# Weight loads in quarters in front of nearly every projection unit, and a running count of equal scores in two halves

## What is computed

```
h = _rmsnorm(x, norm_g[l])
p = h @ w_in[l]
oa = _chunk_band_attention(...) * silu(az)      # A: softmax attention over a band
ob = _hgrn2(...) * silu(bz)                     # B: gated linear recurrence
oc = _dsa(...) * silu(cz)                       # C: indexer, top 256 keys, attention
od = _rwkv7(...) * silu(dz)                     # D: delta-rule state
y = sum over the branches of sigmoid(gate) * (o @ w_branch[l, branch])
x = x + y @ w_out[l]
```

## Time and profile before

| | us |
|---|---|
| median of 3 runs | 2764.34 |
| lowest and highest | 2760.86, 2766.89 |
| time of the profiled execution | 2762.82 |
| its span, first to last instruction | 2761.0 |
| PE busy in the span | 2716.2 |

### The profile page before, as it was taken

How to read it: one execution, slowest core, us unless ns; L and a number is a source line. 1 busy time by engine, 2 the same in 40 slices (tenths; PEclk the granted TensorE clock), 3 DMA queues, 4 the chain that set the end, 5 groups by cost and what they waited for, 6 DMA issues and landing times.

```text
span 2761.0 us, 46225 instructions
## 1 busy us (share of the span) xinstructions
PE 2716.2 (98%) x18624; PEld 1465.9 (53%) x18624; DVE 1595.5 (58%) x3018; ACT 973.2 (35%) x1869; POOL 802.5 (29%) x582
## 2 busy tenths in 40 slices
PE   8999999999999999999999999999999999999999
PEld 4447444466574565544444464544665745755443
DVE  4689876754508732265337898767545178232753
ACT  3455665321224224500124556643112332344001
POOL 3333312411334332133033333124113443321420
PEclk9999999999999999999999999999999999999999
DMA  4221111211111223183142121112111112232731
GB/s 163 68 59 50 46 35 53 70 45 45 47 42 39 63 82 102 32 281 116 41 123 57 46 62 39 36 49 71 50 37 47 46 43 66 70 107 79 246 111 46
DMA packets 135612, 200.90 MB, mean 73 GB/s; under 512 B 8392, under 2 KB 90472, under 8 KB 134632
## 3 DMA queue, kind: packets, MB, share of 16 engines
q1 hardware_dynamic: 116808, 163.86, 19.8%
q10 hardware_dynamic: 18592, 34.09, 3.3%
HBM read 146.53 MB, written 44.59 MB: 69 GB/s over the span
## 4 chain that ended last, share of the span: by engine, by line
PE 44%; DVE 4%; ACT 1%; issue 1%; POOL 0%; DVEq 0%; ACTq 0%
PE ps L498 23%; PE ps L495 4%; PE ps L757 4%; PE ps L771 3%; PE ps L1163 1%; PE ps L1152 1%; PE ps L1498 1%; PE ps L1176 1%; DVE arena L1898 1%; DVE arena L1640 1%; PE ps L2018 1%; PE ps L2112 1%; PE ps L2010 0%; DVE arena L1624 0%; PE ps L1964 0%
## 5 line engine op out<-in xcount | busy, mean ns | idle before, releaser
L498 PE MATMUL ps<-hT,wr 128*128 128x512 f32 x1856 | 858.9, 600 | 3.1 <-PEq L2574 2.8
L498 PEld LDWEIGHTS ps<-hT,wr 128*128 128x128 f32 x1856 | 338.7, 191 | 375.6 <-issue 367.1
L498 PE MATMUL ps<-sums,wr 128*128 128x512 f32 x928 | 438.4, 600 | 1.1 <-ACT gts L568 0.7
L673 POOL TENSOR_TENSOR gts<-gts,wr 128x512 f32<-128x512 f32 x96 | 153.7, 1601 | 621.0 <-ACT wr L549 400.7
L1252 DVE CUSTOM_DVE_ANT_0 arena<-ps,arena 128x640 f32<-128x640 f32 (+7 forms) x128 | 90.5, 707 | 334.1 <-PE ps L1152 317.4
L498 PEld LDWEIGHTS ps<-sums,wr 128*128 128x128 f32 x928 | 167.2, 190 | 180.9 <-issue 171.6
L549 ACT ACTIVATE wr<-ps 128x512 f32<-128x512 f32 x174 | 103.2, 593 | 369.7 <-PE ps L498 324.2
L757 PE MATMUL ps<-xo,arena 128*128 128x512 f32 x512 | 220.1, 592 | 0.0
L498 PE MATMUL ps<-wr 128*128 128x512 f32 x464 | 218.5, 600 | 0.0
L1640 DVE TENSOR_SCALAR_CACHE_REDUCE arena<-arena,sm 128x384 f32<-128x384 uint16 (+7 forms) x256 | 192.8, 809 | 2.2
L642 POOL TENSOR_TENSOR wr<-wr 128x512 f32<-128x512 f32 x57 | 81.2, 1425 | 382.9 <-PE ps L498 347.7
(11 more groups left out here) (321 smaller groups left out, 4139.2 us busy)
## 6 DMA issues: line engine op xcount, KB each, us to landing
wr<-in_w_in SPq DMA_DIRECT2D x36, 1024.0 KB, 5.5
gate_tanh<-gts ACTq DMA_DIRECT2D x128, 256.0 KB, 3.3
arena<-gate_tanh SPq DMA_DIRECT2D x128, 256.0 KB, 2.9
wr<-in_w_in SPq DMA_DIRECT2D x104, 256.0 KB, 2.8
wr<-in_w_in SPq DMA_DIRECT2D x16, 512.0 KB, 3.8
arena<-in_w_branch SPq DMA_DIRECT2D x8, 1024.0 KB, 7.7
wr<-in_w_out SPq DMA_DIRECT2D x8, 1024.0 KB, 7.4
arena<-arena SPq DMA_DIRECT2D x36, 128.0 KB, 2.6
```

The source lines that it names most:

```text
L498: ins = pe.matmul(ap, lhsT=right(u, w_side)[:, kt, :], rhs=left(h_side, kt), start=fresh and kt == 0, stop=kt == half_k - 1, skip_group_ch ...
L673: pool.tensor_tensor(dst, dst, stage_of(u), ALU.add).then_inc(sg("pool_added"), 1)
```

## The change

```diff
             def load_parts(n):
 
                 u = next(u for u in range(len(units)) if n in units[u][1])
-                return 4 if units[u][0] == "gate" and units[u - 1][0] == "gate" else 1
+                return 4 if u >= 2 and n == units[u][1][0] and len(units[u - 1][1]) == 1 else 1
...
-                        key = done if q == 0 else (*fill_done[n - 1][0][:3], q - 1)
+                        key = done if q == 0 else (*fill_done[n - 1][0][:3], 2 * q - 2)
...
-                    ap = jobs.open(pe, key, T)
+                    ap = jobs.open(pe, key, S2[0] if g and u + 1 == len(units) else T)
...
-                    v256 = cbits[:, j:j + 1]
+                    v256, middle = cbits[:, j:j + 1], P * (i + 1) // 2
...
                     elif step == 1:
                         link(dve, dve.tensor_scalar(equal, sc, v256, None, ALU.is_equal))
+                        link(dve, dve.tensor_tensor_scan(sc[:, 0:middle], equal[:, 0:middle], equal[:, 0:middle], 0.0, ALU.add, ALU.max))
                     elif step == 2:
-                        link(dve, dve.tensor_tensor_scan(sc, equal, equal, 0.0, ALU.add, ALU.max))
+                        link(dve, dve.tensor_tensor_scan(sc[:, middle:], equal[:, middle:], equal[:, middle:], sc[:, middle - 1:middle], ALU.add, ALU.max))
```

## The result

| | before | changed |
|---|---|---|
| median, lowest and highest, us | 2765.61 (2760.86 to 2766.99) | 2786.06 (2781.81 to 2788.53) |
| profiled execution, its span | 2762.82, 2761.0 | 2788.53, 2786.7 |
| PE busy | 2716.2 | 2724.8 |
| PE idle in the span | 44.8 | 61.9 |

The changed kernel takes 1.0075 times as long, 95% interval 1.0058 to 1.0093: 20.5 us more between the medians. The direction and the first link of the mechanism are those forecast, the size is twice that forecast: 2775 was said, and 2786.06 lies just under the upper end of the range (2787). The profiled execution is the slowest of the four, 25.7 us over that of before; of these PE's idle time is 17.1 and its busy time 8.6.

A forecast was written before the change was run, and what follows sets the result against it. PE was taken as the bound, busy 2716.2 of 2761.0 us. From 2762.82, +14.8 for stalls at unit ends (7.4 a layer), -0.9 for the scan and -1.5 for the L2010 gap gave 2775.2, forecast 2775, range 2764 to 2787.

The forecast's parts named there:

- The chain: Unit ends: late last quarter delays POOL's t1, its addition, ACT's copy, then PE's bank; 6.1 us against 6.70, 7.1 beside a store.
- two gates with POOL free: Layer 0 gates, product 4 ending at 491.7 and 893.64: load lands in 3.8 beside a store, PE stalls 0.35 us each.
- gate in D: Product 4 ended at 543.35: DVE's 128x2048 addition holds POOL up, so the copy is late and PE stalls 1.55 us.
- B0: Unit end, product 4 ended at 745.23: 3.4 us stall if POOL and DVE take turns, 1.2 if POOL sums in one go.
- gate in B: DVE's row of sums, which held up POOL's addition, would hit t1 too and delay the addition 1.27; stall 0.75 us.
- A's attention: Product 4 ended at 1079.56, store beside the load: ACT's work comes 1.4 late, PE stalls 0.9 to 1.0 us.
- rival 3: ACT's delay spreads: search starts 1.8 us later and PE pays, plus three delays of 0.5; +5 a layer, 2785; chance 0.13.
- C's index: First turns queue behind POOL's later additions, 1.8 us later in sum; DVE idles there several times, so taken as 0.
- C's search: ACT's copies come 0.4 to 0.7 late in three units; even 2 us covered by DVE's 8.81 us idle before the attention.
- The attention of C: One late-ACT end like the one in A's attention, with less in it: stall 0.0 to 0.2 us.
- The gap at L2010: PE's 3.0 us gap beside a 1 MB load, perhaps delayed program fetches; half taken as returning, -1.5 us.
- The scan: Scan halved in C's attention, 2.28 us becoming about 1.2 and 1.2: removes one PE wait; -0.9 us, bounds -1.0 and +0.3.

## Why the prediction was right, and where it was too small

**The chain was right.** The waits of a layer that the prediction named, and what came of them (the wait of PE in layer 0 of the changed kernel, against the term):

| end | term | measured |
|---|---|---|
| two gates with POOL free | 0.35 each | 0.13, 0.43 |
| gate in D | 1.55 | 0.28 + 0.89 |
| B0 | 3.4 | 3.35 |
| gate in B | 0.75 | none |
| A's attention | 1.0 | 1.08 |

Together the waits for L549 and the added ones for L1233 are 11.8 us in both layers, where the sum had 14.8. In B0 the choice between 3.4 and 1.2 was right: the two engines took turns. The lock rule of the Trainium skill (SBUF — State Buffer, section Who interferes with whom) holds in that the loser waits for the whole instruction: POOL's sums of 1.26 took 3.27 and 3.31 beside DVE operations of 2.29 and 3.24.

**The gate in B** failed by its step "the same will hit t1". In the earlier trace rows the addition was shut out by a run of short DVE operations for 3.89 us. In the changed kernel it was the other way round:

```profile
945.91 1.42 POOL L642 TENSOR_TENSOR wr<-wr 128x512 f32<-128x512 f32 x1 [18.25 <-DMA wr<-in_w_in]
946.12 1.75 DVE L1859 TENSOR_TENSOR arena<-arena 128x512 f32<-128x512 f32 x1
947.29 1.71 POOL L673 TENSOR_TENSOR gts<-gts,wr 128x512 f32<-128x512 f32 x1
```

t1 got in at once and DVE's operation waited for it. Which of them gets the port when is not to be read from one instance. (The term had a slip too: it gives the copy 0.70 to spare and then takes off 0.54; with 0.70 it is 0.57, no longer 0.75.)

**The sum was too small, because of what was taken as 0.** Three estimates failed, and rival 3 (ACT's delay spreads into the search and the index, 2785) was the place. That its time is so near the 2786 measured is luck: its own terms, 1.8 and three of 0.5, make 3.3 a layer and 2782, where it says 5 a layer, and the search and the index cost 6.3 in both layers:

- C's index: "DVE idles there several times, and I take 0". POOL's later sums run beside DVE's operations of the index, ACT waits for these, and its copy and PE's next scores come late, 0.44 and 0.68 in a layer, 2.3 in both. In the timeline of the changed kernel, where the same operation of 384 had taken 0.62 before:

```profile
100.97 1.37 POOL L652 TENSOR_TENSOR wr<-wr 128x512 f32<-128x512 f32 x1
101.26 1.50 DVE L1614 SCALAR_TENSOR_TENSOR arena<-arena,sm 128x384 f32<-128x384 f32 x1
102.79 0.60 ACT L549 ACTIVATE wr<-ps 128x512 f32<-128x512 f32 x1 [1.86 <-DVE arena L1614]
102.96 1.13 PE L1499 MATMUL ps<-arena 64*128 64x512 f32 x4 [0.44 <-DVEq L1606]
```

- C's search: "Even 2 us would be covered, since DVE idles 8.81 us between the search and the attention". The search did start 2 us late, and DVE had that room; but PE pays in the search itself, at product 3 of C5, for a copy that ACT gets to late, 2.0 a layer. The prediction looked at which wait a late sum sets free, and not at which DVE operations the later sums fall beside.
- The attention of C: 0.0 to 0.2 was allowed for ACT. POOL's t3 and addition lie beside a two-input operation of the choice there, which takes 1.57 where it took 0.62, and PE waits 0.90 in both layers, 1.7 more than before with what else changed in that row:

```profile
399.64 2.20 POOL L673 TENSOR_TENSOR gts<-gts,wr 128x512 f32<-128x512 f32 x1
...
400.75 1.57 DVE L1387 TENSOR_TENSOR arena<-arena 128x896 f16<-128x896 f16 x1
...
404.76 0.63 PE L1163 MATMUL ps<-con,arena 128*128 128x128 f32 x4 [0.90 <-ACT arena L1219]
```

That is 2.3 + 4.0 + 1.7, 8.0 us. **The clock** is the fourth: the prediction says that PE's busy time stays at 2716, with no term for what follows a wait, and it is 8.6 us more in the profiled execution. Of these 1.7 and 2.7 stand behind B0 and 1.6 in C5, and 1.5 was returned at L2010; 2.7 are the edges of the new waits (a wait of 3.35 moves the next matmul by 3.51, since the end of the matmul ahead is a modelled one), and 1.4 is spread thin. In the fastest of the four runs, 2781.81, the mean clock was 0.999 and in the others 0.997, so part of it comes and goes from one execution to the next.

**The gap at L2010** was taken at half. The whole came back, 3.0 of wait and 1.5 of clock; a gap of 1.1 appeared at L2113 in its stead, for which the profile shows no cause either. Net it is 3.4 us against the 1.5 taken. The prediction's argument against it, that the load was already out for 7 us when the gap came, misreads the trace: it had been out for 4.4 us when the gap began (652.43 to 656.84), and took 7.0 to land.

**The scan**: by itself 0, within the bounds of -1.0 and +0.3, but -6 to -7 beside the late loads, an interaction that no term had. Without it the change would have left the range (2792.31 against 2787), so that the time lies inside is luck as much as the sum. The scan of 3.40 was called an accident; it was the rule, 11 of the 12 widest scans in the six profiles with whole ones, and the 2.28 of layer 1 in the kernel before is the exception.

**The range**: 0.5 for each of seven ends would make 3.5 a layer and an upper end of 21.8 for the waits, where the prediction says 20. In B0 the chain with both sums in one go comes to 1.4, where it says 1.2. Neither changes the account.

The idle time of the profiled execution by these terms: 11.8 + 8.0 - 0.9 (scan) - 3.1 (L2010) + 1.1 (L2113) = 16.9 of the 17.1. Smaller rows that also moved, up and down, are left out of it.

## What to carry to other kernels

A load that is issued later than it is asked for does not cost its own waiting engine alone: list what stands behind the wait in that engine's program order (here an addition that frees a staging buffer), and put work that is ready ahead of it. Then list what the engine's delayed work will run beside, since an operation of VectorE and one of GpSimd that meet can hold each other up (0.9 to 1.1 us each time ahead of C's search), and PE may be told of it 16 us later. A wait of PE of 2 to 6 us can cost 1.6 to 3 more in clock, or nothing; no length seen here settles it, and one of 1.64 had the low clock too.

## What the runs showed of the hardware

- A fetch of instructions came 2.6 us late beside a transfer of 1 MB, and PE stood 2.98 us; with the transfer cut in four, 0.34. The cut of this one block took 4.8 us off the median, the cut of all of them 2.9 (the two intervals overlap).
- After a wait of 2.2 to 6.1 us the granted clock was 0.56 to 0.62 in the mean of the next 4 to 7 us, or did not fall: 2.20 and 2.21 at the same matmul, 2.92 twice, and 2.76 to 2.78 at the same matmul in fourteen profiles went both ways. Of two waits at L2011, 1.64 and 1.65 us, one had it.
- What a stretch of low clock costs at once is not always what it costs in the end: the 1.6 us lost in C5 had come back some 40 us later, 1.0 of them out of waits that PE has there at the full clock.
- Six two-input operations of DVE took 9.05 us beside GpSimd's operations and 4.90 alone. Single-input ones (TENSOR_SCALAR on int32) were held up as well: 128x512 took 1.52 beside a sum and 0.42 alone.
